# A mixture-of-experts layer on one core: expert blocks of 32 places on quarters of the matmul array in place of 64 places on halves

## The reference, cut to what matters

```python
eid = gsel[:, None] * EXPERTS_PER_GROUP + ei          # two experts for a token, 32 in all
xin = x_pad[buf_tok].reshape(nblk, MOE_BLOCK, D)      # the tokens' rows, sorted by expert, padded

def expert_block(args):
    xb, e = args
    return (jax.nn.silu(xb @ w1[e]) * (xb @ w3[e])) @ w2[e]      # w1, w3: 1024 x 512; w2: 512 x 1024

out = jax.ops.segment_sum(y * buf_w[:, None], buf_tok, num_segments=T + 1)[:T]
```

## Time and profile before

| | us |
|---|---|
| median of 3 runs | 1649.77 |
| lowest, highest | 1649.05, 1652.81 |
| the profiled execution's own time | 1650.04 |
| its span, first to last instruction | 1648.4 |
| PE busy in the span | 1564.9 (95%) |
| mean granted TensorE clock | 0.988 of full speed |

### The profile page before, as it was taken

The page is one execution under the profiler, slowest core; times in us unless marked ns, Lnnn a source line. Parts: engine busy times, 40 slices in busy tenths (PEclk is TensorE's granted clock), DMA queues, the critical chain, the costliest instruction groups (busy, mean ns, idle before and its releaser), DMA issues.

```text
span 1648.4 us, 21863 instructions
## 1 busy us (share of the span) xinstructions
PE 1564.9 (95%) x7698; PEld 848.1 (51%) x7699; DVE 560.9 (34%) x1542; ACT 346.8 (21%) x859; POOL 300.6 (18%) x431
## 2 busy tenths in 40 slices
PE   7999998999999999998999999799899999999986
PEld 4554544444444444444444555566466666666652
DVE  4210004766566656654222354511011111111115
ACT  3000002443343443433000111111111111111113
POOL 2000001322222222222001001221121212121114
PEclk9999999999999999998999999999999999999997
DMA  9214621553111110103443821699999989999928
GB/s 236 67 56 62 125 78 58 166 181 114 45 32 26 45 33 26 46 13 90 161 136 103 357 107 74 235 416 419 419 419 418 386 352 407 416 421 417 415 85 306
DMA packets 135914, 328.42 MB, mean 199 GB/s; under 512 B 40046, under 2 KB 80398, under 8 KB 126640
## 3 DMA queue, kind: packets, MB, share of 16 engines
q1 hardware_dynamic: 117472, 297.98, 49.5%
q0 software_dynamic: 9984, 17.62, 3.2%
q10 hardware_dynamic: 8400, 12.07, 2.1%
HBM read 276.09 MB, written 55.25 MB: 201 GB/s over the span
## 4 chain that ended last, share of the span: by engine, by line
PE 83%; DVE 7%; DMA 5%; issue 2%; ACT 2%; POOL 1%; SPq 1%; POOLq 0%; ACTq 0%; DVEq 0%
PE PS L856 17%; PE PS L707 12%; PE PS L591 11%; PE PS L870 9%; PE PS L745 7%; PE PS L780 7%; PE PS L693 4%; PE PS L654 4%; PE PS L673 4%; PE PS L586 3%; DMA WA<-w 2%; PE PS L833 2%; DMA BA<-hn_d,ids 1%; POOL WA L1532 1%; PE PS L573 1%
## 5 line engine op out<-in xcount | busy, mean ns | idle before, releaser
L707 PE MATMUL PS<-WA 128*128 128x512 f32 x512 | 255.0, 611 | 2.2 <-ACT WA L967 1.6
L856 PE MATMUL PS<-WA,BA 128*64 128x256 f32 x2048 | 227.6, 379 | 2.9 <-DMA WA<-w 1.5
L856 PEld LDWEIGHTS PS<-WA,BA 128*64 128x64 f32 x2048 | 173.9, 137 | 63.9 <-issue 17.3
L591 PE MATMUL PS<-WA,BA 128*128 128x512 f32 x416 | 180.1, 593 | 2.9 <-DVE WA L1090 2.9
L1450 POOL TENSOR_SCALAR BA<-BA,rin,gates 128x640 f32<-128x640 f32 (+7 forms) x128 | 99.6, 781 | 270.8 <-DVE rin L1209 270.8
L1364 DVE SCALAR_TENSOR_TENSOR BA<-BA,PS 128x256 f32<-128x256 f32 x46 | 19.4, 422 | 340.8 <-ACT BA L1029 340.8
L591 PEld LDWEIGHTS PS<-WA,BA 128*128 128x128 f32 x416 | 78.6, 190 | 99.6 <-issue 96.2
L673 PEld LDWEIGHTS PS<-ident,BA 128*128 128x128 f32 x648 | 79.4, 144 | 94.1 <-issue 86.6
L870 PE MATMUL PS<-WA,BA 128*64 128x512 f32 x512 | 116.9, 597 | 9.7 <-DVE BA L1374 8.7
L707 PEld LDWEIGHTS PS<-WA 128*128 128x128 f32 x512 | 84.6, 190 | 78.4 <-issue 67.6
L957 ACT ACTIVATE BA<-PS,ngm 128x640 f32<-128x640 f32 (+7 forms) x128 | 89.9, 702 | 130.5 <-DVE ngm L1187 126.1
(11 more groups left out here) (249 smaller groups left out, 1548.4 us busy)
## 6 DMA issues: line engine op xcount, KB each, us to landing
WA<-w SPq DMA_DIRECT2D x66, 2048.0 KB, 25.3
BA<-w SPq DMA_DIRECT2D x30, 2048.0 KB, 27.6
rows_d<-WA SPq DMA_DIRECT2D x8, 2048.0 KB, 9.5
rows_d<-BA ACTq DMA_DIRECT2D x92, 128.0 KB, 6.8
WA<-w_in SPq DMA_DIRECT2D x16, 512.0 KB, 5.6
gates_d<-WA SPq DMA_DIRECT2D x32, 256.0 KB, 2.4
WA<-gates_d SPq DMA_DIRECT2D x8, 1024.0 KB, 5.4
BA<-w_in SPq DMA_DIRECT2D x26, 256.0 KB, 6.1
```

Of the source, the lines that this page charges most:

```text
L591: mm = pe.matmul(PS[:, j % 4, :], ws[:, c % 6, k, :], hnT[:, k, 512 * h:512 * h + 512], start=(k == 0), stop=(k == KT - 1))
L707: mm = pe.matmul(PS[:, 6, :], gw[:, j, k, :], hnT[:, k, 512 * hf:512 * hf + 512], start=(k == 0), stop=(k == KT - 1))
L856: mm = pe.matmul(PS[DH * h:DH * h + DH, bank, 0:256], xT[:, k, :], w[par][:, k, 256 * h:256 * h + 256], start=(k == 0), stop=(k == KT - 1))
```

## The change

`SLOTS` becomes 32, and an expert has at least two blocks: `max(2, ceil(rows / 32))`. On the counts above these are 78 blocks (three for each of the fourteen experts with more than 64 rows, two for each other) in place of 46.

- PE: a block's four products (W1 and W3, each in two halves of 256 columns) go to the four quarters of the array, into one PSUM bank, and the product with W2 as four quarters of 256 columns. The product with W2 of a block is moved behind the next block's product with W1 and W3 (`put_out` after `hidden_sums`). One transpose of `hv` in place of two, two of `xin` in place of four. One register load for an expert in place of two.
- Rows: whole rows of 1024 numbers are gathered into one of two buffers of 32 partitions (`rows_in`); DVE spreads each row as four quarters over the 128 partitions of `xin` (`spread_rows`, four copies), and PE transposes that. Row numbers are fetched into a column of `ids` for each buffer, with one DMA for a block.
- ACT: the result is copied out of PSUM by four copies of 32 x 256 in place of one of 128 x 512, into one of two buffers, and stored with one DMA in place of two.
- SP: the load of W1 now waits for the same count as that of W3 (`mm13`).
- Ahead of the loop: the rows of block 1 come from the same list as those of block 0, so that the second list (`mark`, `place1`) and its 32 small matmuls go.

The diff, cut to its core:

```diff
-SLOTS = 64
-MAXB = NE + 2 * SEQ // SLOTS
+SLOTS = 32
+MAXB = 2 * NE + 2 * SEQ // SLOTS - 4
+FIRST = 2 * SLOTS
...
+    rows_in = [BA[0:SLOTS, 1152:2176], BA[0:SLOTS, 2176:3200]]
+    xin = ba(8192, 8448)
+    xT = ba(9216, 9472, "p (k n) -> p k n", k=KT)
+    xT_first = PS[:, 7, 0:KT * SLOTS].rearrange("p (k n) -> p k n", k=KT)
+    xT_out = xT.rearrange("p (q c) n -> p c q n", c=2)
+    xT_ps = PS[:, 7, 0:KT * SLOTS].rearrange("p (c q n) -> p c q n", c=2, q=4)
+    th = BA[0:FIRST, 9728:9984]
+    hu = BA[FIRST:2 * FIRST, 9984:10240]
+    hv = ba(10240, 10368)
+    hT = ba(10496, 10624)
+    ysb = [BA[0:SLOTS, 10752:11776], BA[0:SLOTS, 3200:4224]]
...
-                sp.wait_ge(S[("mm1", "mm3", "y_ps")[j]], used)
+                sp.wait_ge(S[("mm13", "mm13", "y_ps")[j]], used)
...
-        def expert(e, nth, par):
...
+        def hidden_sums(b, par, landed):
+            pe.wait_ge(S["xT_evac"], pe.snap(b + 1))
+            for n in range(2):
+                pe.wait_ge(S[f"we{3 * par + n}"], landed)
+            for k in range(KT):
+                for q in range(4):
+                    w = (W1, W3)[q // 2][par]
+                    mm = pe.matmul(PS[SLOTS * q:SLOTS * q + SLOTS, 0, 0:256], xT[:, k, :],
+                                   w[:, k, 256 * (q % 2):256 * (q % 2) + 256], start=(k == 0), stop=(k == KT - 1))
+            mm.then_inc(S["mm13"], 1)
+            pe.wait_ge(S["x_free"], pe.snap(b + 2))
+            turn_rows()
+        def put_out(n_done, par, landed):
+            pe.wait_ge(S["hT_done"], n_done)
+            pe.wait_ge(S["y_evac"], n_done)
+            pe.wait_ge(S[f"we{3 * par + 2}"], landed)
+            for j in range(2):
+                for h in range(2):
+                    for n in range(4):
+                        mm = pe.matmul(PS[SLOTS * n:SLOTS * n + SLOTS, 3, 0:256], hT[:, FIRST * j + SLOTS * h:FIRST * j + SLOTS * h + SLOTS],
+                                       W2[par][:, 2 * h + j, 256 * n:256 * n + 256],
+                                       start=(j == 0 and h == 0), stop=(j == 1 and h == 1))
+            mm.then_inc(S["y_ps"], 1)
+        def turn_hidden(b):
+            pe.wait_ge(S["hid_done"], pe.snap(b + 1))
+            pe.transpose(PS[:, 2, 0:P], hv, ident[:, :]).then_inc(S["hT_ps"], 1)
+        def expert(e, lo, par, landed, landed_before):
+            hi = pe.value_load(starts_i[0:1, bass.ds(e + 1, 1)], min_val=2, max_val=MAXB)
+            hidden_sums(lo, par, landed)
+            if landed_before is not None:
+                put_out(lo, (par - 1) % NW, landed_before)
+            turn_hidden(lo)
+            with pe.Fori(lo + 1, hi) as b:
+                hidden_sums(b, par, landed)
+                put_out(b, par, landed)
+                turn_hidden(b)
+            return hi
...
+        end = pe.snap(pe.value_load(starts_i[0:1, 0:1], min_val=0, max_val=0))
+        for e in range(NW):
+            end = expert(e, end, e, 16, None if e == 0 else 16)
+        with pe.Fori(1, NE // NW) as e3:
+            end = pe.value_load(starts_i[0:1, bass.ds(e3 * NW, 1)], min_val=2, max_val=MAXB)
             for par in range(NW):
-                expert(e3 * NW + par, e3 + 1, par)
+                end = expert(e3 * NW + par, end, par, pe.snap(e3 * 16 + 16), pe.snap(e3 * 16 if par == 0 else e3 * 16 + 16))
+        end = pe.value_load(starts_i[0:1, NE - NE % NW:NE - NE % NW + 1], min_val=2, max_val=MAXB)
         for e in range(NE - NE % NW, NE):
-            expert(e, e // NW + 1, e % NW)
+            end = expert(e, end, e % NW, 16 * (e // NW + 1), 16 * ((e - 1) // NW + 1))
+        put_out(end, (NE - 1) % NW, 16 * ((NE - 1) // NW + 1))
...
-            act.wait_ge(S["mm1"], b + 1)
-            nc.scalar.activation(th[:, :], PS[:, 0, 0:256], ACT.Tanh, scale=0.5).then_inc(S["tanh_done"], 1)
-            act.wait_ge(S["x_tr"], b + 3)
-            act.wait_ge(S["mm3"], b + 1)
+            act.wait_ge(S["mm13"], b + 1)
+            nc.scalar.activation(th, PS[0:FIRST, 0, 0:256], ACT.Tanh, scale=0.5).then_inc(S["tanh_done"], 1)
+            act.wait_ge(S["x_tr"], b + 1)
             nc.scalar.copy(xT_out, xT_ps).then_inc(S["xT_evac"], 1)
-        def put_rows(b):
-            act.wait_ge(S["y_ps"], b + 1)
-            nc.scalar.copy(ysb[:, :], PS[:, 3, :]).then_inc(S["y_evac"], 1)
-            act.wait_ge(S["y_evac"], b + 1)
+        def put_rows(n_done, side, first):
+            act.wait_ge(S["y_ps"], n_done)
+            for n in range(4):
+                y = nc.scalar.copy(ysb[side][:, 256 * n:256 * n + 256], PS[SLOTS * n:SLOTS * n + SLOTS, 3, 0:256])
+            y.then_inc(S["y_evac"], 1)
+            act.wait_ge(S["y_evac"], n_done + 1)
+            act.dma_start(rows_d[bass.ds(first, SLOTS), :], ysb[side]).then_inc(S[f"y_st{side}"], 16)
+        gate_and_rows(0)
+        gate_and_rows(1)
+        put_rows(1, 0, 0)
+        with act.Fori(1, act.snap(total - 1), 2) as b:
             for n in range(2):
-                act.dma_start(rows_d[bass.ds(b * SLOTS, SLOTS), 512 * n:512 * n + 512],
-                              ysb[DH * n:DH * n + DH, :]).then_inc(S["y_st"], 16)
-        gate_and_rows(0)
-        put_rows(0)
-        with act.Fori(1, total) as b:
-            gate_and_rows(b)
-            act.wait_ge(S["y_st"], act.snap(b * 32))
-            put_rows(b)
-        act.wait_ge(S["y_st"], act.snap(total * 32))
...
+        def spread_rows(side):
+            for q in range(4):
+                rows = dve.tensor_copy(xin[SLOTS * q:SLOTS * q + SLOTS, :], rows_in[side][:, 256 * q:256 * q + 256])
+            rows.then_inc(S["x_free"], 1)
...
+        def hidden(b):
+            dve.wait_ge(S["mm13"], b + 1)
             dve.wait_ge(S["tanh_done"], b + 1)
-            dve.scalar_tensor_tensor(hu[:, :], th[:, :], 1.0, PS[:, 0, 0:256], ALU.add, ALU.mult).then_inc(S["hu_done"], 1)
+            dve.scalar_tensor_tensor(hu, th, 1.0, PS[0:FIRST, 0, 0:256], ALU.add, ALU.mult).then_inc(S["hu_done"], 1)
             dve.wait_ge(S["hu_done"], b + 1)
-            dve.wait_ge(S["mm3"], b + 1)
-            halves = [dve.snap(b * 2 + 1), dve.snap(b * 2 + 2)]
             for j in range(2):
                 part = slice(P * j, P * j + P)
-                dve.scalar_tensor_tensor(hv[:, part], hu[:, part], 0.5, PS[:, 1, part], ALU.mult, ALU.mult) \
-                    .then_inc(S["hid_done"], 1)
-            for j in range(2):
-                dve.wait_ge(S["hT_ps"], halves[j])
-                dve.tensor_copy(hT[:, j, :], PS[:, 2 + 2 * j, 0:P]).then_inc(S["hT_done"], 1)
+                product = dve.scalar_tensor_tensor(hv[FIRST * j:FIRST * j + FIRST, :], hu[:, part], 0.5,
+                                                   PS[FIRST:2 * FIRST, 0, part], ALU.mult, ALU.mult)
+            product.then_inc(S["hid_done"], 1)
+        def take_hidden(b):
+            dve.wait_ge(S["hT_ps"], b + 1)
+            dve.tensor_copy(hT, PS[:, 2, 0:P]).then_inc(S["hT_done"], 1)
+        with dve.Fori(0, total, 2) as b:
+            for side in range(2):
+                now = dve.snap(b + side)
+                hidden(now)
+                dve.wait_ge(S[f"x_blk{side}"], dve.snap(b * 8 + 32))
+                dve.wait_ge(S["x_tr"], dve.snap(b + side + 1))
+                spread_rows(side)
+                take_hidden(now)
...
+        with pool.Fori(2, total + 2, 2) as b:
+            for side in range(2):
+                pool.wait_ge(S[f"ids_in{side}"], pool.snap(b * 8))
+                pool.wait_ge(S["x_free"], pool.snap(b + side - 1))
+                pool.wait_ge(S[f"x_blk{side}"], pool.snap(b * 8))
+                pool.sem_inc(S["rows_due"], 1)
+                g.tensor_copy(ids[0:SLOTS, 2 + side:3 + side], ids[0:SLOTS, side:side + 1]).then_inc(S["ids_held"], 1)
+                pool.wait_ge(S["ids_held"], pool.snap(b + side - 1))
+                pool.sem_inc(S["rows_due"], 1)
+                g.indirect_dma_start(rows_in[side], None, hn_d[:, :],
+                                     bass.IndirectOffsetOnAxis(ap=ids[0:SLOTS, 2 + side:3 + side], axis=0),
+                                     bounds_check=SEQ - 1, oob_is_err=False).then_inc(S[f"x_blk{side}"], 16)
+                load_ids(side, pool.value_load(block_row_i[0:1, bass.ds(b + side + 2, 1)], min_val=0, max_val=NE * SEQ + 2 * FIRST))
```

More of the change, by code:

```diff
@@ L798, in first_rows @@
             pe.wait_ge(S["sel_done"], m + 1)
[L799 to L802, removed]
+            return pe.matmul(PS[0:FIRST, 0, 0:2], sel[:, m, :], tok[:, m, :],
+                             start=(m == 0), stop=(m == TT - 1), skip_group_check=True)
         def keep_busy(count):
@@ L820, in _ @@
         pe.wait_ge(S["h2_done"], TT)
[L821 to L827, removed]
         keep_busy(10)
         def turn_rows():
-            for c in range(4):
+            for c in range(2):
                 mm = pe.transpose(PS[:, 7, P * c:P * c + P], xin[:, P * c:P * c + P], ident[:, :])
             mm.then_inc(S["x_tr"], 1)
-        pe.sem_inc(S["x_tr"], 1)
```

(26 more changed lines are left out.)

143 lines of the change are left out of this document (48 added, 95 removed).

## The result

| us | before | after |
|---|---|---|
| median (12 runs each) | 1650.55 | 1656.18 |
| lowest, highest | 1648.17, 1652.81 | 1653.32, 1662.97 |
| the profiled execution's own time | 1650.04 | 1654.65 |
| PE's last product with W2 ends | 1603 | 1607.5 |

The ratio is 1.0039, with a 95% interval of 1.003 to 1.0049: slower by 0.4%, where 1615 us was forecast. The forecast's mechanism on PE came out, and the time did not.

What follows compares the result with a forecast made beforehand. PE bounds the kernel, with DMA close behind. Reload at 1071 plus 480 us of DMA ends loads at 1551; PE ends at 1570 for 1603, so 1650.04 - 33 = 1617, taken as 1615 us; range 1598 to 1680, likeliest case to 1640.

Steps and rivals of the forecast that it cites:

- Quarters run four at a time: PE's products: four array parts each work through their own records, 54 ns per 256-column record, 6.1 us a block.
- Rival 1: PE's matmul records keep program order, two at a time: 108 ns each, block 11.3 us, time 1986 us; chance 0.19.
- the forecast's reading of the order: PE: strict program order would let only one matmul's second record and the next's first run together.
- Cover on ACT, DVE and for rows and numbers: Expert loop: ACT 2.8 us and DVE 2.1 to 3.0 of 6.1; row and number rounds fit at their medians.
- Rival 2: The round for rows or numbers, not PE, decides the expert loop: 1622 to 1678 us; chance 0.08.
- DMA then bounds: Expert phase: with PE faster, DMA's 201.0 MB set the end, loads finishing at 1551 us.
- At 419 GB/s: DMA rate assumed for the changed expert phase: 201.0 MB in 480 us.
- 32 packets where it had 128: Row gather in the expert loop: said to have fewer packets, an argument against slow rounds for rows.
- First reload at 1071: SP's first weight reload, after expert 0's third block: 1071 us, 4 later than before the change.
- Rival 3: PE's clock drops while waiting at two-block experts: block 5.2 us longer at 1.2 GHz, price up to 5 us; no separate chance.
- Rival 4: Nothing gained in the expert phase, because DMA is full already: time within 0.2% of before; chance 0.04.
- the forecast's 1570: PE's end after the last expert's blocks: 1570 us, for 1603 before.

Runs made afterwards that it cites:

- e7: Changed kernel, but each weight load from expert 3 on brings only its first eighth (results not the layer's): 1608.39 us.
- e1: Changed kernel with one more wait on POOL: the next row numbers are fetched only once the gather has landed: 1760.89 us, ratio to the kernel before 1.068.
- e2: Changed kernel with rows gathered as quarters of 1 KB into all 128 partitions, one DVE copy spreading them: 1631.43 us, ratio to the kernel before 0.9881.
- e9: Changed kernel with rows gathered as halves of 2 KB into partitions 0 to 31 and 64 to 95: 1629.01 us (kernel before: 1649.52).
- e5: Changed kernel with rows gathered as halves of 2 KB into partitions 0 to 63, two number loads a block: 1656.48 us.
- e4: Changed kernel with gathers of 16 numbers of each row in place of 1024 (results not the layer's): 1612.95 us.

## Why the prediction was wrong

- **Quarters run four at a time: right.** 56 and 58 ns for 54, a block 6.09 us for 6.1. Rival 1 is refuted: by it only two would run together, and a record would stay at 108 ns. What falls is the forecast's reading of the order that the Trainium skill ("TensorE: Matmul & The Clock Gate", What overlaps and what doesn't) states, as one between the two records of a matmul and the next matmul's. The order of whole matmuls these runs leave open: the four of a group may still start and end in turn, some 7 ns apart.
- **Cover on ACT, DVE and for rows and numbers: right**, after block 2: beside weights and the changes of expert PE's waits hold no row above 1.5 us. In e7 PE runs without one wait on rows after it. Rival 2 came only where e1 made it.
- **DMA then bounds: right. At 419 GB/s: wrong, and this is the step that failed.** I took the rate over from a kernel whose gather writes all 128 partitions, into one whose gather writes 32. It became 396.5 GB/s between 1110 and 1500 us, and 394 over the whole 471 us. That made 29 of the 37.6 us. The fault was to count bytes only (8.4 MB "before and after") and to ask of the new gather how many packets it has, not where they land. The count itself was off: for "32 packets where it had 128" the DMA records show 4 KB packets in both, 1414 before and 1400 after between 1110 and 1500 us. e2 and e9 give the rate back (415, 417), and e5 does not.
- **First reload at 1071: mis-sized, 1076.76.** I took the numbers' issue (1051.10) over from before; it waited 8.49 us for the scatter, which the new order issues 3.7 us later. PE stood 6.5 us for block 2, as forecast, but everything lay later. Then block 0's product with W2 took 3.16 us in place of 1.93: after the standstill the granted clock was 0.57 (1068.9 to 1072.6 us).
- **The changes of expert: left out.** 31 standstills, 22.9 us in all when DMA doesn't bound (e7), and part of the 2.8 after the last landing (PE waits 1.15 and 0.27 at two changes, and 1.45 for the last `hT`).
- **Rival 3, the clock:** the granted clock was 0.95 on average from 1400 to 1566 us, for 1.00 before; the product that came after a wait of 2.83 us at 1512.10 took 5.35 us in place of 3.66, at a granted clock of 0.68. DMA covered it, since PE waited for weights again at 1547.72.
- **Rival 4:** nothing of PE's gain was left, but not because DMA was full already. With the rate given back and all else kept, e2's PE ends 17.4 us after the forecast's 1570, and this is the other terms: 8 for the first reload (1078.97), 6.7 for the rate up to expert 29 (448.7 us for 442, at 414 GB/s from the first reload on), 2.7 at the end. (e4's 1612.95 us is no proof of the forecast, since 8.4 MB are gone in it, some 20 us.)

The rows of before could have given the bound: the share of DMA was 1.02 in the earlier trace rows, so any 5% that DMA loses goes straight into the end: by an estimate from the forecast's own 480 us, 24 us.

## What to carry to other kernels

When a change frees one engine and leaves DMA as the bound, the DMA rate itself must be forecast anew: look at which partitions each transfer writes, the small ones too, since 8 MB of gathers into partitions 0 to 31 (or 0 to 63) cost 5% of the rate of 182 MB of weights beside them. Spread a narrow gather so that it writes both below and above partition 64. And do the sum of a loop with a term for each time it changes over.

## What the runs showed of the hardware that was not expected

- Partitions 0 to 63 are no better a target than 0 to 31 (393 and 397 GB/s in all), while 0 to 31 with 64 to 95 is as good as all 128 (417 and 415).
- The slow-down falls mostly on the other queue's packets, and on some of them: 16 KB packets from 620 to about 650 ns on average, with the median at 618 in e2 and 615 in the changed kernel, but 15% above 700 ns, where e2 has 8 packets of 6019.
- Writing rows into partitions 0 to 31 cost 5% of the rate; storing 10.2 MB out of partitions 0 to 31, in e9 as in the changed kernel, left it at 417 GB/s.
- A scatter of row numbers lands in 2.1 us at its median, and took 7.9 when two loads of 2 MB had been issued 0.2 us before it.
- Four quarters of the array take 56 ns for a float32 record of 32 x 256, where halves take 108 for one of 64 x 256.
